# Feed-forward up projections: high and low activation parts streamed as one 512-column operand, sums in two halves of a bank

## What is computed

```python
# layers 0 and 1 ("A"), D_FF = 2816
h = rms_norm(x, pre_ffn_norm[l])
gate, up = jnp.split(jnp.einsum('bsd,df->bsf', h, ffn_w_gate_up[l]), 2, axis=-1)
f = jnp.einsum('bsf,fd->bsd', jax.nn.silu(gate) * up, ffn_w_down[l])
x = x + rms_norm(f, post_ffn_norm[l])
...
# layers 2 to 5 ("B"), D_FF_2 = 4096
hm = _rms_norm(x, mlp_norm[i])
x = x + jnp.square(jax.nn.relu(hm @ mlp_w_up[i])) @ mlp_w_down[i]
```

## Time and profile before

| | us |
|---|---|
| median of 3 runs | 2084.98 |
| lowest and highest of them | 2083.89, 2086.36 |
| span of the profiled execution (first to last instruction) | 2085.7 |
| one chunk of layer A, start of a down step to the next | 16.98 |
| one chunk of layer B | 22.42 |
| feed-forward chunks in all | 22 of A, 32 of B |

### The profile page before, as it was taken

How to read it: one execution, slowest core, us unless ns; L and a number is a source line. 1 busy time by engine, 2 the same in 40 slices (tenths; PEclk the granted TensorE clock), 3 DMA queues, 4 the chain that set the end, 5 groups by cost and what they waited for, 6 DMA issues and landing times. The chain is left out here.

```text
span 2085.7 us, 28577 instructions
## 1 busy us (share of the span) xinstructions
PE 1956.9 (94%) x11232; PEld 1689.4 (81%) x11232; DVE 1167.0 (56%) x1741; ACT 921.3 (44%) x1256; POOL 237.2 (11%) x301
## 2 busy tenths in 40 slices
PE   5899999899989989899999999999989999989998
PEld 4666999775689988778998879998858998868997
DVE  3556555674655568665445465445675444775443
ACT  3445433444443346464344454444215443664432
POOL 0400000040000002000010000103960100100000
PEclk8968999996899999799999999999999999999999
DMA  6602555551045555314554535554304555424551
GB/s 193 216 1 71 171 190 183 164 175 40 21 160 189 184 202 175 132 40 163 201 171 172 181 108 173 169 196 167 116 0 160 174 190 202 161 82 165 198 191 71
DMA packets 183954, 308.64 MB, mean 148 GB/s; under 512 B 18438, under 2 KB 67132, under 8 KB 183868
## 3 DMA queue, kind: packets, MB, share of 16 engines
q1 hardware_dynamic: 182572, 304.24, 43.3%
q10 hardware_dynamic: 1296, 3.23, 0.5%
HBM read 306.39 MB, written 1.05 MB: 147 GB/s over the span
## 5 line engine op out<-in xcount | busy, mean ns | idle before, releaser
L1297 DVE TENSOR_TENSOR w_lo<-raw,w_hi 128x2048 fp32r<-128x2048 f32 (+2 forms) x290 | 647.5, 2264 | 308.5 <-ACT w_hi L890 307.8
L890 ACT ACTIVATE w_hi<-raw 128x2048 fp32r<-128x2048 f32 (+2 forms) x290 | 533.1, 1876 | 111.3 <-PE tr L1789 63.8
L1787 PE MATMUL acc<-w_hi,aux_hi 128*128 128x512 f32 x688 | 269.4, 392 | 12.2 <-DVE aux_lo L1747 12.2
L1788 PE MATMUL acc<-w_lo,aux_hi 128*128 128x512 f32 x688 | 269.0, 391 | 0.0
L1789 PE MATMUL acc<-w_hi,aux_lo 128*128 128x512 f32 x688 | 268.3, 390 | 0.0
L1787 PE MATMUL up<-hT_hi,w_hi 128*128 128x256 f32 x864 | 245.9, 285 | 8.1 <-ACT proj L1228 5.1
L1787 PE MATMUL acc<-w_hi,hT_hi 128*128 128x512 f32 (+2 forms) x608 | 239.4, 394 | 10.3 <-DVE w_lo L1297 8.7
L1788 PE MATMUL up<-hT_lo,w_hi 128*128 128x256 f32 x864 | 244.9, 283 | 0.0
L1787 PE MATMUL tr<-hT_hi,w_hi 128*128 128x256 f32 x864 | 244.9, 283 | 0.0
L1789 PE MATMUL up<-hT_hi,w_lo 128*128 128x256 f32 x864 | 244.9, 283 | 0.0
L1788 PE MATMUL tr<-hT_lo,w_hi 128*128 128x256 f32 x864 | 244.5, 283 | 0.0
(11 more groups left out here) (320 smaller groups left out, 2679.2 us busy)
## 6 DMA issues: line engine op xcount, KB each, us to landing
raw<-in_mlp_w_up SPq DMA_DIRECT2D x64, 1024.0 KB, 6.3
raw<-in_mlp_w_down SPq DMA_DIRECT2D x64, 1024.0 KB, 5.5
raw<-in_ffn_w_gate_up SPq DMA_DIRECT2D x88, 512.0 KB, 4.7
raw<-in_ffn_w_down SPq DMA_DIRECT2D x22, 1024.0 KB, 5.2
raw<-in_w_in SPq DMA_DIRECT2D x16, 1024.0 KB, 7.0
raw<-in_sb_w_in SPq DMA_DIRECT2D x12, 1024.0 KB, 5.3
raw<-in_moba_w_in SPq DMA_DIRECT2D x12, 1024.0 KB, 5.3
raw<-in_nsa_w_in SPq DMA_DIRECT2D x10, 1024.0 KB, 6.4
```

The lines of the kernel that those rows point to most:

```text
L890: nc.scalar.activation(w_hi[:, p0.slot, 0:p0.floats], raw[:, p0.slot, 0:p0.floats], ACT.Copy)\
L1297: nc.vector.tensor_tensor(w_lo[:, p0.slot, 0:m], raw[:, p0.slot, 0:m], f32(w_hi[:, p0.slot, 0:m]), ALU.subtract).then_inc(sem["lo_ready"], 1)
L1787: nc.tensor.matmul(dst, hi, whi, start=first, stop=False)
L1788: nc.tensor.matmul(dst, hi, wlo, start=False, stop=False)
```

## The change

The two activation parts become one tile, `hT`, with the high part's 256 positions and the low part's 256 side by side for each of the 8 feature tiles. A hidden block is now made of pairs: `w_hi` is loaded once and 512 columns are streamed (high and low part) into a whole bank, then `w_lo` is loaded and 256 columns (high part) are streamed into the left half. The left half then holds high by high plus high by low, the right half the third product. ScalarE copies the right halves out of the banks (L1230, twice), and VectorE adds the left halves to them.

Layer A: the adds (L1751, twice) write `gate_scaled` and `up_scaled`; VectorE then multiplies the gate by the row factors (L1753), GpSimd the up part (L863). ScalarE's split of the next first up piece moves from the middle of hidden(c) to behind the two copies. Layer B: the adds (L1729) are followed on VectorE by `max(r, 0) * r` (L1735 of the changed kernel), which takes the place of ScalarE's Relu and GpSimd's squares; VectorE's splits of the next pieces move behind it. New semaphores carry the new order.

```diff
-        hT_hi = sb("hT_hi", [P, KT, S], F32R)
-        hT_lo = sb("hT_lo", [P, KT, S], F32R)
+        hT = sb("hT", [P, KT, 2, S], F32R)
+        hT_hi, hT_lo = hT[:, :, 0, :], hT[:, :, 1, :]
...
@@ GpSimd @@
-                if ph.kind == "ffn" and ph.variant == "B":
+                if ph.kind == "ffn" and ph.variant == "A":
+                    pool.wait_ge(sem["rows_kept"], n["rows_kept"] + 1)
                     for i, steps in ffn_schedule(ph, pool):
...
-                            nc.gpsimd.tensor_tensor(ffn_r2[:, W * j:W * j + W], r, r, ALU.mult)\
+                        nc.gpsimd.tensor_tensor(pairs(up_scaled), pairs(up_scaled),
+                                                bc(rstd_rows.unsqueeze(1), [P, 2, S]), ALU.mult)\
+                            .then_inc(sem["u_scaled"], 1)
...
@@ ScalarE @@
+                    act.wait_ge(sem["piece_used"], along(i, steps, used))
+                    if steps[0] > 0:
+                        act.wait_ge(sem["r2_ready"], along(i, steps, lambda c: n["r2_ready"] + ph.kt // 2 * c))
+                    for j, half in enumerate((ffn_r[:, 0:W], ffn_r[:, W:2 * W]) if ph.variant == "B" else
+                                             (gate_scaled, up_scaled)):
+                        nc.scalar.activation(pairs(half), right_sums[j], ACT.Copy).then_inc(sem["half_kept"], 1)
+                    if not early:
                         next_piece(0)
...
@@ VectorE, B @@
+                        for j in range(2):
+                            dve.wait_ge(sem["half_kept"], along(i, steps, lambda c: n["half_kept"] + 2 * c + j + 1))
+                            half = pairs(ffn_r[:, W * j:W * j + W])
+                            nc.vector.tensor_tensor(half, left_sums[j], half, ALU.add).then_inc(sem["r_ready"], 1)
...
+                            nc.vector.scalar_tensor_tensor(out=ffn_r2[:, W * j:W * j + W], in0=r, scalar=0.0, in1=r,
+                                                           op0=ALU.max, op1=ALU.mult).then_inc(sem["r2_ready"], 1)
...
@@ VectorE, A @@
+                        for j, (half, name) in enumerate(((gate_scaled, "g_ready"), (up_scaled, "u_ready"))):
+                            dve.wait_ge(sem["half_kept"], along(i, steps, lambda c: n["half_kept"] + 2 * c + j + 1))
+                            nc.vector.tensor_tensor(pairs(half), left_sums[j], pairs(half), ALU.add).then_inc(sem[name], 1)
+                        dve.wait_ge(sem["g_ready"], along(i, steps, lambda c: n["g_ready"] + c + 1))
+                        nc.vector.tensor_tensor(pairs(gate_scaled), pairs(gate_scaled),
+                                                bc(rstd_rows.unsqueeze(1), [P, 2, S]), ALU.mult)\
+                            .then_inc(sem["g_scaled"], 1)
...
@@ TensorE @@
-                                last = three(hidden_sums[a], w_hi[:, slot, at:at + P], w_lo[:, slot, at:at + P],
-                                             hT_hi[:, kk, :], hT_lo[:, kk, :], kk == 0, kk == KT - 1)
+                                nc.tensor.matmul(hidden_banks[a], w_hi[:, slot, at:at + P],
+                                                 hT[:, kk, :, :].rearrange("p j s -> p (j s)"), start=kk == 0, stop=False)
+                                last = nc.tensor.matmul(hidden_banks[a][:, 0:S], w_lo[:, slot, at:at + P],
+                                                        hT_hi[:, kk, :], start=False, stop=kk == KT - 1)
```

More of the change, by code:

```diff
@@ L249, in make_plan @@
             phases.append(Phase("ffn", variant="A", first=first, n=n, per=3, ups=2, downs=1, kt=2, row=2 * l + 1,
[L250 removed]
+                                counts={"diag_ready": 1, "rows_done": 1, "rows_kept": 1, "g_ready": n, "u_ready": n,
+                                        "g_scaled": n, "u_scaled": n, "half_kept": 2 * n, "r_ready": n, "r2_ready": n,
                                         "act_hi": n, "act_lo": n, "tile_done": 1, "y_sq": 2 * TT, "x_written": 2 * TT}))
@@ L453, in first_second_block @@
         cmp_pos = vecT[:, 1, 24:88].rearrange("p (j l) -> p j l", j=2)
-        hidden_sums = [(up, tr)[a // 2][:, a % 2, 0:S] for a in range(4)]
-        wide_sums = [bank[:, :, 0:S] for bank in (up, tr)]
+        hidden_banks = [(up, tr)[a // 2][:, a % 2, :] for a in range(4)]
+        left_sums, right_sums = ([bank[:, :, S * j:S * j + S] for bank in (up, tr)] for j in range(2))
         ffn_r = proj[:, 0, 0:4 * S]
@@ L857, in _ @@
                             .then_inc(sem["diag_ready"], 1)
-                if ph.kind == "ffn" and ph.variant == "B":
+                if ph.kind == "ffn" and ph.variant == "A":
+                    pool.wait_ge(sem["rows_kept"], n["rows_kept"] + 1)
                     for i, steps in ffn_schedule(ph, pool):
-                        if steps[0] > 0:
-                            pool.wait_ge(sem["act_lo"], along(i, steps, lambda c: n["act_lo"] + 2 * c))
-                        for j in range(2):
-                            pool.wait_ge(sem["r_ready"], along(i, steps, lambda c: n["r_ready"] + 2 * c + j + 1))
-                            r = ffn_r[:, W * j:W * j + W]
-                            nc.gpsimd.tensor_tensor(ffn_r2[:, W * j:W * j + W], r, r, ALU.mult)\
-                                .then_inc(sem["r2_ready"], 1)
+                        pool.wait_ge(sem["u_ready"], along(i, steps, lambda c: n["u_ready"] + c + 1))
+                        nc.gpsimd.tensor_tensor(pairs(up_scaled), pairs(up_scaled),
+                                                bc(rstd_rows.unsqueeze(1), [P, 2, S]), ALU.mult)\
+                            .then_inc(sem["u_scaled"], 1)
                 n.advance(ph)
@@ L1219, in next_piece @@
                             split_hi(pieces_at(ph.per + j), i)
-                    early = ph.variant == "B" and steps[0] == 0
+                    early = steps[0] == 0
                     if early:
                         next_piece(0)
-                        next_piece(1)
-                    if ph.variant == "B":
-                        act.wait_ge(sem["piece_used"], along(i, steps, used))
-                        for j in range(2):
-                            nc.scalar.activation(pairs(ffn_r[:, W * j:W * j + W]), wide_sums[j], ACT.Relu)\
-                                .then_inc(sem["r_ready"], 1)
-                        if not early:
-                            next_piece(0)
-                    else:
+                        if ph.variant == "B":
+                            next_piece(1)
+                    act.wait_ge(sem["piece_used"], along(i, steps, used))
[5 more added lines that the diff above has]
+                    if not early:
                         next_piece(0)
-                        act.wait_ge(sem["g_ready"], along(i, steps, lambda c: n["g_ready"] + c + 1))
+                    if ph.variant == "A":
+                        act.wait_ge(sem["g_scaled"], along(i, steps, lambda c: n["g_scaled"] + c + 1))
                         nc.scalar.activation(gate_silu, gate_scaled, ACT.Silu).then_inc(sem["r_ready"], 1)
-                    if not early:
+                    if ph.variant == "A" or not early:
                         next_piece(1)
@@ L1721, in ffn @@
                     if ph.variant == "B":
-                        next_piece(0)
+                        if steps[0] == 0:
+                            next_piece(0)
+                            next_piece(1)
+                        dve.wait_ge(sem["piece_used"], along(i, steps, used))
+                        for j in range(2):
+                            dve.wait_ge(sem["half_kept"], along(i, steps, lambda c: n["half_kept"] + 2 * c + j + 1))
+                            half = pairs(ffn_r[:, W * j:W * j + W])
+                            nc.vector.tensor_tensor(half, left_sums[j], half, ALU.add).then_inc(sem["r_ready"], 1)
+                        if steps[0] > 0:
+                            dve.wait_ge(sem["act_lo"], along(i, steps, lambda c: n["act_lo"] + 2 * c))
+                        for j in range(2):
+                            dve.wait_ge(sem["r_ready"], along(i, steps, lambda c: n["r_ready"] + 2 * c + j + 1))
+                            r = ffn_r[:, W * j:W * j + W]
+                            nc.vector.scalar_tensor_tensor(out=ffn_r2[:, W * j:W * j + W], in0=r, scalar=0.0, in1=r,
+                                                           op0=ALU.max, op1=ALU.mult).then_inc(sem["r2_ready"], 1)
+                        if steps[0] > 0:
+                            next_piece(0)
+                            next_piece(1)
                     if ph.variant == "A":
```

18 lines of the change are left out of this document (6 added, 12 removed).

## The result

The changed kernel takes **2112.2 us** (median of 4 runs, 2103.8 to 2119.5); four more runs gave 2107.5 (2100.0 to 2118.0). Against the runs of the kernel before on the same chip (2085.67) the ratio is 1.0122, 95% interval 1.0093 to 1.0151; the second set gave 1.0099 (1.0063 to 1.0135). It is slower, and outside the predicted range. The profiled run took 2110.88 us with a span of 2109.1, so 23.3 us more than the span before.

The account below looks back on a forecast made before the run. The feed-forward was taken as bound by PE's columns plus a fixed cost per matmul. B at -9.9 and A at +3.9 and +5.8 summed to -0.2 us, giving 2084.8 us, own range 2080 to 2089, with rivals 2075 to 2094.

Parts of the forecast that it names:

- The gain: Hidden steps: a triple costs 0.360 us, a pair 0.347, so 0.013 saved 32 times, 0.416 us per hidden step.
- rival 2: Hidden-step pairs save less; at 6.7 ns per pair the time is 2095.4 us; chance 0.10.
- First to second hidden step: Between hidden(0) and hidden(1), added work delays PE's release: +0.85 us four times in B, +0.64 twice in A.
- rival 3: Clock falls behind hidden(0) in six layers, +9.6 us, 2094.4; chance 0.08, shared with longer stalls in A.
- Layer B, the other steps: B's remaining hidden steps: a cover of 3 us hides the added VectorE work, so the cost is nothing.
- Layer A, the stall: A's loop: w_lo waits behind the copies and GpSimd's scaling; PE stalls 0.67 us per boundary, nine boundaries per layer.
- D: The start of a down step, from which the prediction counts times.
- X: The moment ScalarE gets the sums; taken as D + 0.36 us in the loop of layer A.
- The ends of the A layers: Last down steps of A come later through the delayed w_lo; A totals +3.9 us (first layer) and +5.8 (second).
- The mixers at nothing: Everything outside the six feed-forward stretches was predicted to change by 0 us.

Follow-up runs that it names:

- fill: The changed kernel plus eight 512-column matmuls behind the first hidden step, whose sums nobody reads: 2104.48 us, ratio 1.0078.
- three256: The changed kernel with three 256-column matmuls instead of the pair in seven of eight feature tiles: 2118.91 us.
- early: The changed kernel with ScalarE's w_hi split of the next first up piece put back before the copies in layers A: 2100.21 us in one run.
- second pair: Second profiles of both kernels, each run once more unedited: 2081.09 us for the kernel before, median 2107.51 for the changed one.
- a_only: The kernel before with the change in the two layers A alone, layers B as before: 2108.55 us, ratio 1.0102.

## Why the prediction was wrong, step by step

The prediction summed a gain and waits to -0.2 us; every wait was there, but the gain was half of the forecast and the waits cost more. By span less 0.40 of the half-clock time the changed kernel loses 2020.6 - 2008.0 = 12.6 us, and the 30.6 us more at half clock cost another 12.2. In the profiles the forecast missed 23.6 us (+23.4 measured). From the lengths of the steps I estimate some 10.5 of them for the pair, 5 for the stalls in A, 4.5 for the clock behind hidden(0), and 3.5 for the ends of the layers A, the down steps of B and the mixers.

- **The gain, "a triple costs 3 x 0.120, a pair 0.227 + 0.120": failed.** Each price was right for its own row, but the rows had equal neighbours on both sides. Mixed, a pair takes 0.3528 in B: 7 ns saved instead of 13, 0.222 per hidden step instead of 0.416. In A the price held in 8 of 18 hidden steps (0.347) and failed in the others. This is rival 2 (6.7 ns, 2095.4 us), to which I gave 0.10 with the reason that "the forms of this case show 13.3"; none of those rows had the form that the change makes. That its 6.7 ns fits is luck: it took a fixed cost of 6.7 from matmuls of 30 weight columns, while here the 13.3 stayed and up to 6.7 more were paid per pair. The Trainium skill's 2.5 ns per warm matmul ("TensorE: Matmul & The Clock Gate", the section on the 56 ns that are not 53.3) was below what any form here showed: 6.7 with 30 weight columns, 13.3 with 128, and 16.4 where widths are mixed.
- **First to second hidden step: right in B, the clock missed.** The wait of PE was forecast at 2.1 and about 2.2 us and was 2.17 and 2.20. The +0.85 came out as 0.30 + 2 x 0.222 = +0.74. But "1.61 us did nothing, and 2.1 is nearer to that" was a guess between two rows and fell: 2.2 us halved the clock in all twelve layers A and in 11 of the 24 layers B of the seven profiles without fill. In B that cost 1.5 to 1.7 us each; in A the first two hidden steps are 1.0 to 1.7 us longer than with the fill. In the profiled run that was 3 of the 6 places of rival 3.
- **Layer B, the other steps: cover right.** No wait of PE appears in B's loop; the chunk is 22.23 instead of 22.00, 0.19 of it the pair. The down step is 10.943 long instead of 10.908; in `three256`, which differs only in the hidden steps' matmuls and ends them with equal neighbours, it is 10.909, so the 0.035 come with the mixed pairs ahead of it.
- **Layer A, the stall: mechanism right, size too small.** Forecast 6.14 from down step to hidden step, measured 6.34. `w_lo` ended at D + 6.11 instead of D + 5.93. ScalarE was 0.07 earlier than thought, but GpSimd's end was at X + 3.67 instead of X + 3.43: its operation takes at least 1.15 after VectorE's scaling (257.26 to 258.41), not 1.04 less the overlap. `w_lo` then ended 2.15 after it (2.14 predicted). The rest: PE starts 0.24 behind the release, and the first pair of the step is slower (0.42; 11.37 for the hidden step against 11.29 in B). With the smaller gain that is 0.19 + 0.18 + 0.03 + 0.08 = 0.48 for the chunk shown, which is 0.73 - 0.25. Not every chunk divides so: `w_lo` ends at D + 6.1 in each but the first layer's first (6.5); in the loop of the second layer PE starts up to 0.5 behind it (6.48 us from down step to hidden step in the mean, 6.37 in the first layer), and more hidden steps have the low price (11.24 us in the mean, 11.33 in the first). The sum stays 0.47 to 0.49 per chunk; over 18 chunks 8.6 us. What makes PE start later there was not tried. That GpSimd and VectorE exclude each other when both read two operands from SBUF was taken from the earlier trace rows and held; the Trainium skill ("SBUF — State Buffer", section on SBUF's two separate sides) says the same of the port pair that they share, and in `early` the 2.15 us came again.
- **The ends of the A layers: mechanism right, size too small.** The last down piece was issued at D + 6.13 instead of D + 3.88 (+2.25, predicted +2.08). The bias transfers behind it took 11.52 us to issue instead of 10.53, which was not foreseen, and the last down step began 2.8 us later after its D than before. Why they took longer no run shows. In the second layer PE's wait was 4.04, predicted 3.7, and the step behind it ran at half clock as predicted, but for 5.9 us, so that it became 2.75 us longer (8.47 instead of 5.72) and not 1.6. In the first layer the clock cost only 0.3 us more than before (7.56 instead of 7.28), since 2.8 us of the fall lie in the wait.
- **The mixers at nothing: a term without a reason, and open.** They took 0.8 us more in the first pair of profiles, with single stretches ahead of the feed-forwards at +4.4 and -6.1 us, and 13.5 us more in the second pair. Whether the change itself makes the mixers run longer at half clock stays open: in the mixers of the two profiles of each kernel it was 191 and 172 us before, 196 and 213 after.

## What to carry to other kernels

A saving read from a distance between equal instructions is a saving of that pattern only: time the pattern that the change makes, above all where the whole gain is a few ns times thousands. Moving work from PE to engines that looked idle lengthened the waits of PE, and the long ones (2.2 us and more) were often paid twice, once as idle time and once at half clock. Where VectorE's splits feed PE, as here, operations with two SBUF operands on GpSimd cost PE's time (17.7 us per chunk with, 17.1 without). The fastest version here was B changed and A as before (`b_only`, 2081.57, ratio 0.9972), or both changed with the early split, no GpSimd and the fill (2080.97, ratio 0.9985, interval up to 1.0010); only the first is shown to beat the kernel before.

## What the runs showed of the hardware

- An `F32R` matmul with 128 weight columns costs columns / 2.4 GHz plus 0.0133 us between equally wide neighbours (256 or 512). Where 512 alternates with 256, a pair takes 0.3467 us, which is the same cost, or 0.3533, through a whole hidden step; in the loops of B it was always the second. Where 512 alternates with 384, 0.4067 or 0.4133.
- PE idle for 2.2 us halved its clock for 3.4 us in 23 of 36 places, and in 8 of 18 in the versions with other widths; eight matmuls in the gap, which left 0.3 us of it, in 0 of 20.
- VectorE's 128x2048 subtraction ends 2.15 us after the end of a GpSimd operation that it meets, in 60 of 60 chunks of three profiles (changed kernel, `a_only`, `early`), whenever it started: 2.89 us long when started 0.74 before GpSimd's end, 3.39 when 1.24 before.
- One program's mean clock over its first 198 us was 0.84 in one execution and 0.89 in the next.
